# The last eight tap positions of a 31-tap convolution summed on GpSimd instead of VectorE

## The reference, cut to what matters

```python
ca, cb = jnp.split(cv, 2, axis=-1)          # 256 channels each
u = ca * jax.nn.sigmoid(cb)
u = causal_dwconv(u, cv_dw_w) + cv_dw_b      # CV_K = 31 taps, one weight per channel and tap
y_cv = jax.nn.silu(layernorm(u, cv_ln_g, cv_ln_b))
return jnp.concatenate([y_attn, y_dn, y_cv], axis=-1) @ w_out
```

## Time and profile before

| | |
|---|---|
| time, median of 3 runs | 1764.81 us (1764.64 to 1769.44) |
| the profiled execution | 1773.58 us, of which the span from first to last instruction is 1771.5 us |
| busy | TensorE 1600.8 us (90%), VectorE 1188.2 (67%), ScalarE 809.9 (46%), GpSimd 60.5 (3%) |
| mean granted TensorE clock | 0.928 of full speed |
| token mixer of layer 0, tile 9 to the output projection | about 164 to 331 us |
| the same of layer 1 | about 926 to 1094 us |

### The profile page before, as it was taken

How to read it: one execution, slowest core, us unless ns; L and a number is a source line. 1 busy time by engine, 2 the same in 40 slices (tenths; PEclk the granted TensorE clock), 3 DMA queues, 4 the chain that set the end, 5 groups by cost and what they waited for, 6 DMA issues and landing times.

```text
span 1771.5 us, 22310 instructions
## 1 busy us (share of the span) xinstructions
PE 1600.8 (90%) x8914; PEld 1243.6 (70%) x8914; DVE 1188.2 (67%) x1376; ACT 809.9 (46%) x936; POOL 60.5 (3%) x49
## 2 busy tenths in 40 slices
PE   6899978897999998998999788958999999999992
PEld 5467756675888886884677556657888888888882
DVE  4677785477666664444657854256888888888884
ACT  2344226323222222122452254246777777777773
POOL 6200000000000000000000000020000000000001
PEclk9799988798999998998999977968999999999996
DMA  7253220153656554431211100538999999999974
GB/s 312 94 175 116 81 96 1 38 201 95 183 177 186 179 183 136 139 137 36 71 50 43 54 1 4 184 120 294 381 390 392 393 380 392 392 393 384 391 292 154
DMA packets 93718, 341.89 MB, mean 193 GB/s; under 512 B 9904, under 2 KB 14000, under 8 KB 90928
## 3 DMA queue, kind: packets, MB, share of 16 engines
q1 hardware_dynamic: 91312, 332.09, 52.1%
q0 software_dynamic: 2304, 8.39, 1.3%
HBM read 318.42 MB, written 22.02 MB: 192 GB/s over the span
## 4 chain that ended last, share of the span: by engine, by line
PE 79%; DVE 11%; ACT 4%; issue 2%; DMA 2%; POOL 1%; SPq 0%; DVEq 0%; ACTq 0%; POOLq 0%
PE ps L599 33%; PE ps L1101 10%; PE ps L1099 9%; PE ps L1100 9%; DVE scr L1520 5%; PE ps L585 2%; DVE scr L1517 1%; PE ps L914 1%; PE ps L571 1%; ACT whi L1133 1%; PE ps L888 1%; PE ps L745 1%; PE ps L628 1%; PE ps L578 1%; DVE wlo L1527 1%
## 5 line engine op out<-in xcount | busy, mean ns | idle before, releaser
L599 PE MATMUL ps<-hhi,whi 128*128 128x512 f32 x768 | 324.1, 422 | 8.1 <-DVE hlo L1520 8.0
L1527 DVE TENSOR_TENSOR wlo<-raw,whi 128x1024 fp32r<-128x1024 f32 (+1 forms) x114 | 147.1, 1291 | 252.0 <-ACT whi L1133 250.1
L599 PE MATMUL ps<-hhi,wlo 128*128 128x512 f32 x768 | 309.8, 403 | 0.0
L599 PE MATMUL ps<-hlo,whi 128*128 128x512 f32 x768 | 308.5, 402 | 0.0
L1517 DVE TENSOR_TENSOR wlm<-rawm,hlo 128x2048 fp32r<-128x2048 f32 x120 | 274.8, 2291 | 42.5 <-ACT hlo L1414 40.8
L1133 ACT ACTIVATE whi<-raw 128x1024 fp32r<-128x1024 f32 (+1 forms) x114 | 125.7, 1103 | 358.4 <-PE ps L599 357.3
L1414 ACT ACTIVATE hlo<-rawm 128x2048 fp32r<-128x2048 f32 x120 | 230.0, 1918 | 81.5 <-PE ps L1101 81.5
L599 PEld LDWEIGHTS ps<-hhi,whi 128*128 128x128 f32 x768 | 147.9, 193 | 77.3 <-issue 31.4
L1100 PE MATMUL ps<-wlm,xgh 128*128 128x512 f32 x480 | 188.3, 392 | 0.0
L599 PEld LDWEIGHTS ps<-hlo,whi 128*128 128x128 f32 x768 | 147.9, 193 | 35.9 <-issue 3.9
L599 PEld LDWEIGHTS ps<-hhi,wlo 128*128 128x128 f32 x768 | 147.5, 192 | 35.3
(11 more groups left out here) (291 smaller groups left out, 2388.5 us busy)
## 6 DMA issues: line engine op xcount, KB each, us to landing
rawm<-in_wm SPq DMA_DIRECT2D x360, 512.0 KB, 7.4
raw<-in_w SPq DMA_DIRECT2D x98, 512.0 KB, 3.5
adah<-in_ada SPq DMA_DIRECT2D x56, 512.0 KB, 4.3
scr<-in_ada SPq DMA_DIRECT2D x20, 1024.0 KB, 5.8
raw<-in_w SPq DMA_DIRECT2D x16, 704.0 KB, 4.1
xs<-scr SPq DMA_DIRECT2D x15, 512.0 KB, 5.4
xg<-xs SPq DMA_DIRECT2D x15, 512.0 KB, 7.4
ys<-yb SPq DMA_DIRECT2D x15, 512.0 KB, 9.1
```

The source lines that it names most:

```text
L599: ins = pe.matmul(ps[:, b, :], a, r[:, k0 + k, :], start=(start and first and k == ks[0] and n == 0), stop=(stop and last and k == ks[-1] ...
L1527: dve.tensor_tensor(wlo[:, slot, 0:width], raw[:, slot, 0:width], whi[:, slot, 0:width].bitcast(F32), ALU.subtract).then_inc(sem("lo_ready ...
```

## The change

`LATE_TAPS` = 23 splits the taps. VectorE keeps the taps d = 0 to 22 (46 instructions a layer), in a list of that length and with calls `taps(m)` of other sizes. GpSimd takes d = 23 to 30. It can't multiply and add with a tensor in one instruction as written here, so each tap beyond the first is a product into unit 16 (`tensor_scalar` with the channel's weight) and an addition to unit 15 (`CP`), for both sides in turn: 16 products and 14 additions a layer, each behind a semaphore `late_tap` of the ones it depends on. It starts when both PSUM banks of tiles 8 and 9 are free, so when `UT` is whole, and in layer 0 also when the last modulation group of this stretch is summed, since units 15 and 16 are its buffer. VectorE adds `CP` to `CY` once, for both sides together, in half step 1, behind its own last tap. The sync queue waits for that addition (`late_added`) before it loads modulation group 13 into units 15 and 16, ahead of the output projection's tiles.

```diff
--- before.py
+++ after.py
@@ -337,6 +337,7 @@
         KT, VT = side(unit(21), 0), side(unit(21), 1)
         ON = side(unit(21), 1)
         UT, CY, ZT = unit(22), unit(23), unit(24)
+        CP = unit(15)
         ROTT = side(unit(25), 0)
         VTOK = side(unit(25), 1).rearrange("p (n d) -> p n d", n=4)
         R8, LN8, G8, Z8, T8, X8 = (side(unit(n), a)[0:8] for n, a in ((24, 0), (24, 1), (25, 0), (25, 1), (23, 0), (22, 0)))
@@ -347,6 +348,7 @@
         mx, negm, rsum, esk, rden = ([small[:, 80 + 16 * n + 8 * a:88 + 16 * n + 8 * a] for a in range(2)] for n in range(5))
         nsink = small[:, 160:168]
         STEPS = 16
+        LATE_TAPS = 23
 
         def scale_of(k):
             return cole[:, :, k, :].rearrange("p m h -> p h m").unsqueeze(3).broadcast_to([P, 4, 4, 64])
@@ -442,6 +444,8 @@
                     load_ada(G_IN + 3)
             for n in range(DC):
                 load_tile(N_IN_TILES + n + 2)
+                if n == 1:
+                    sp.wait_ge(sem("late_added"), 1)
                 load_ada(G_GATE + n)
             for i in range(FC):
                 for j in range(2):
@@ -539,6 +543,27 @@
                                         ALU.add, ALU.min))
                 pool.tensor_scalar(ang[:, n, :], ang[:, n, :], -float(np.float32(3.1415925)), None, ALU.max)\
                     .then_inc(sem("ang_ready"), 1)
+
+            for layer in range(DEPTH):
+                if layer == 0:
+                    pool.wait_ge(sem("ada_acc"), summed(G_IN + 3))
+                for j in range(2):
+                    pool.wait_ge(sem(f"bank_free{j}"), U_IN[layer] + 5)
+                for d in range(LATE_TAPS, CV_K):
+                    for n in range(2):
+                        o, src = side(CP, n), side(UT, n)
+                        w = PR("cconv", (layer * 2 + n) * CV_K + CV_K - 1 - d)
+                        at = (2 * (CV_K - LATE_TAPS) - 1) * layer * 2 + 4 * (d - LATE_TAPS) - 2 * (d > LATE_TAPS)
+                        first = d == LATE_TAPS
+                        if not first:
+                            pool.wait_ge(sem("late_tap"), at - 1 + n)
+                        out = o if first else side(unit(16), n)
+                        pool.tensor_scalar(out[:, d:], src[:, :S - d], w, None, ALU.mult).then_inc(sem("late_tap"), 1)
+                    for n in range(2):
+                        if d > LATE_TAPS:
+                            o = side(CP, n)
+                            pool.wait_ge(sem("late_tap"), at + 1 + n)
+                            pool.tensor_tensor(o[:, d:], o[:, d:], side(unit(16), n)[:, d:], ALU.add).then_inc(sem("late_tap"), 1)
 
             pool.wait_ge(sem("xs_cleared"), 16 * NB)
             pool.wait_ge(sem("slots_ready"), 1)
@@ -1703,7 +1728,7 @@
                     link(tt(q, q, cosb[:]))
                     mark(tt(q, q, ROTT, ALU.add), "roped")
 
-                tap_list = [(d, n) for d in range(CV_K) for n in range(2)]
+                tap_list = [(d, n) for d in range(LATE_TAPS) for n in range(2)]
 
                 def taps(m):
 
@@ -1714,7 +1739,7 @@
                         if d == 0:
                             ins = dve.tensor_scalar(o, src, w, PR("cb", layer * 2 + n), ALU.mult, ALU.add)
                         else:
-                            dve.wait_ge(sem(f"tap{n}"), CV_K * layer + d)
+                            dve.wait_ge(sem(f"tap{n}"), LATE_TAPS * layer + d)
                             ins = stt(o[:, d:], src[:, :S - d], w, o[:, d:])
                         ins.then_inc(sem(f"tap{n}"), 1)
 
@@ -1781,16 +1806,13 @@
                         ada_groups((G_IN + 1,))
                     if layer == 0 and t in (6, 9):
                         ada_groups((G_IN + (2 if t == 6 else 3),))
-                    if t >= 10:
-                        taps(3 if t == 13 else 4 if t != 15 else 6)
+                    if 10 <= t < 17:
+                        taps(3 if t == 13 else 4)
                     if t == 13:
                         solved()
                         taps(1)
                     if t == 14:
                         queries_less_absorbed()
-                        taps(2)
-                    if t == 17:
-                        taps(2)
 
                 def maxima(i):
 
@@ -1834,10 +1856,14 @@
                 for i in range(STEPS):
                     maxima(i)
                     if i < 2:
-                        taps(6 if i == 0 else 2 * CV_K)
+                        taps(3)
                     if i == 1:
                         for n in range(2):
-                            dve.wait_ge(sem(f"tap{n}"), CV_K * v)
+                            dve.wait_ge(sem(f"tap{n}"), LATE_TAPS * v)
+                        dve.wait_ge(sem("late_tap"), 2 * (2 * (CV_K - LATE_TAPS) - 1) * v)
+                        ins = tt(cy[:, :, LATE_TAPS:], cy[:, :, LATE_TAPS:],
+                                 CP.rearrange("p (a s) -> p a s", a=2)[:, :, LATE_TAPS:], ALU.add)
+                        mark(ins, "late_added")
                         dve.sem_inc(sem("taps_done"), 1)
                     if i in (2, 4, 6):
                         state(3 + i // 2)
```

## The result

The changed kernel takes 1773.9 us (median of 13 runs, 1770.7 to 1783.25); the kernel before took 1767.24 us beside it (13 runs, 1764.16 to 1772.67). The ratio is 1.0036, with a 95% interval of 1.0021 to 1.0051: 6.4 us slower, between 3.7 and 9.0. The time is inside the range of 1756 to 1775 us and 8 us above the forecast of 1766: the change is a small loss, where "the two cancel" was the likeliest case. Of these 8 us 2.4 are the base: the forecast was added to 1764.81, a median of three runs, where thirteen give 1767.24. One execution of a later experiment (the products-only kernel: 2328.74 us at a granted clock of 0.628, where the others had 0.93) was slow as a whole and is left out of its ratio.

A forecast was written before the change was run, and what follows sets the result against it. VectorE's taps ahead of the mean's matmuls were taken to bound the kernel. A gain of 11.6 us against 12.0 of contention and 1 for the clock made +1.4 on 1764.81, so 1766 us, range 1756 to 1775.

The forecast's parts named there:

- the two cancel: Whole kernel: 12.0 us lost to contention, 11.6 gained, 1 for TensorE's clock, net +1.4 us, 1766 us; chance 0.45.
- What bounds the kernel: End of input projection: VectorE's 18 taps hold the mean's matmuls; added VectorE time between tile 9 and the copy costs fully.
- What it removes: 16 of 62 taps per layer; nine delay the second maximum, 0.64 us each: 5.8 us a layer, 11.6 in all.
- GpSimd and the sync queue: GpSimd's 43 us of work per layer ends at about 212 to 225, wanted at 259; the sync queue's wait costs nothing.
- What GpSimd costs VectorE: From tile 9 on, GpSimd's additions and products delay VectorE: 6.8 us in layer 0, 5.2 in layer 1, 12.0 in sum.
- the overlay of the two orders: GpSimd's order laid over VectorE's up to the copy: 5.7 us in layer 0, 4.2 in layer 1.
- the upper end of 18: Contention on VectorE if its single-operand work suffers too: some 18 us instead of 12.
- The clock: TensorE's longer waits ahead of the turned keys lower its clock: between 0 and 2 us, say 1.
- Rival (c): Slower by the clock: layer 0 loses its early clock return behind the mean, +8.0 us, 1773 us; chance 0.23.
- case (a): The likeliest case, loss 12.0 us against gain 11.6, plus 1 for the clock: +1.4 us, 1766 us; chance 0.45.
- Rival (b): Contention mostly misses: additions fall beside PSUM reads and transposes, loss about 5 us, net -6.6, 1753 to 1758 us; chance 0.25.
- rival (d): Every GpSimd instruction blocks for its whole length, products costing 1.3 us when met: 20 us over (a), 1786 us; chance 0.07.

The follow-up runs named there:

- products-only kernel: Changed kernel without GpSimd's 14 additions a layer, all 16 products kept: 1763.78 us, ratio 0.9974 to the kernel before.
- the filler: 22 unread TensorE matmuls a layer around the attention's half steps: 1765.53 us (ratio 0.9983) in the kernel before, 1763.78 us (0.9965) in the changed kernel.
- additions-only kernel: Changed kernel with GpSimd's products cut to four a layer, then 14 additions in a row: 1780.77 us, ratio 1.0069 to the kernel before.
- the moved taps: Kernel before, all 62 taps on VectorE, 12 a layer moved forward: 1760.01 us, ratio 0.9945; with 22 unread TensorE matmuls a layer 1750.97 us, ratio 0.9898.

## Why the prediction was right or wrong

**What bounds the kernel**: right. VectorE's taps held the mean's matmul, and a microsecond more on VectorE ahead of the copy delays the copy.

**What it removes**: right, 12.0 us where the sum had 11.6. The second maximum came 5.8 us a layer earlier in the sum, 5.7 in the trace of layer 0, and the mean's matmul 6.0 in both layers; it was then released by TensorE's own L939 (the old L914), as said, and neither the last three taps nor the new addition (1.18 us, with 1.2 expected) shows in the time.

**GpSimd and the sync queue**: right that nobody waits. GpSimd ended at 216.3 us; it took 50 us where the prediction had 43 undisturbed.

**What GpSimd costs VectorE**: the mechanism and the two prices held (0.79 to 0.86 us for 0.9, 0.24 to 0.30 for 0.25 to 0.3), and the term was too small all the same, 15.3 us for 12.0. Layer 0's copy came 7.6 us later, not 5.7; layer 1's 4.5, for 4.2; behind each copy 1.6 us, for 1.1 and 1.0. The step that failed is the overlay of the two orders: I let five additions and five products meet something ahead of layer 0's copy, and six additions and ten products had run by then. Most of layer 0's miss of 1.9 us sits on two instructions that layer 1 doesn't have, the operations of tile 10 on the tables `cosb` and `sinb`. In the order of time of before:

```profile
175.35 0.54 DVE L1773 TENSOR_SCALAR cosb<-cosb,cst 128x512 f32<-128x512 f32 x1
175.92 0.49 DVE L1774 TENSOR_SCALAR sinb<-sinb,cst 128x512 f32<-128x512 f32 x1
```

Beside two additions they took 1.44 and 1.33 us (L1798, L1799), 1.7 us more. They read one tensor from SBUF each; the prediction counts them among the work on two operands and names single-operand work only as its upper end, so it doesn't say whether the 5.7 us contain them. VectorE's read of PSUM at 201.67, beside additions, took the same 1.22 us as before. A value between 12 and the upper end of 18 would have been the better middle.

**The clock**: too small, at 1 us for both layers. Rival (c) named its sign, L888 behind the mean at 2.00 us in layer 0, and the profile has it (267.99); it had also named the opposite, layer 1 winning, and that came too, in the same execution. These two are a swap of 5.4 against 6.4 us, and another trace of the change has neither. What stayed is elsewhere, in the stretch from the outputs to the square sum: in both layers together 125.7 to 125.8 us in the three traces of the change, 123.0 and 121.7 in the two of before. The clock and busy time of layer 1's, before and then after (window, its us, then the busy time and count of each engine, the granted clock, DMA share and GB/s):

```profile
1049.50:1106.50 57.00, 48.63 (x329) 38.24 (x327) 24.28 (x44) 28.71 (x60) 0.00 (x0) 0.82 0.02 2
```
```profile
1047.30:1107.10 59.80, 51.18 (x323) 39.41 (x322) 24.03 (x44) 28.86 (x60) 0.00 (x0) 0.77 0.01 2
```

The work is the same (VectorE 24.3 and then 24.0 us, ScalarE 28.7 and 28.9), the clock is 0.77 for 0.82, and 57.0 x 0.82 = 46.7 and 59.8 x 0.77 = 46.0 are nearly the same number of cycles: these 2.8 us are clock. The change adds and removes no computation in this stretch. That it only shifts how TensorE arrives there is argued, not shown; for it speaks that with the filler both kernels have 0.82 in layer 1 and the difference is gone.

**The sum.** 15.3 - 12.0 = +3.3 us from contention and gain; -1.6 from a stretch at lowered clock in layer 0's solve to scores (37.3 to 35.7), which both traces of before have and none of after. On average of three traces after and two before, another 3.5 us lie in the last two stretches and 0.6 in layer 1's copy to solve (one trace of before had 21.6 there, the others of both kernels the slower step). Together 5.8, for 6.4 measured. That lies between case (a), +1.4, and rival (c), +8.0, nearer to (c). Of the miss of 5.0 us, 2.9 are contention (3.3 more of it than predicted, less 0.4 more gain); 1.5 are the clock's by these traces (-1.6, 3.5 and 0.6 make 2.5, with 1 predicted), and 0.6 lie outside what the stretches show. Two terms were too small in the same direction; the time is inside the range because that reached 9 us above the forecast. That the clock's part comes from the change rests on five traces and on the pair with the filler matmuls; how often an execution of either kernel falls into which pattern stays open. Rival (b) needed additions to miss, and ahead of the copies few did; rival (d) is refuted by the products-only kernel (0.24 to 0.30 us a product, not 1.0).

## What to carry to other kernels

Work handed to an engine whose instructions hold up those of the bound one isn't free where that one has no slack: price it by kind of instruction (here about 0.8 us for each two-input addition and 0.3 for each one-input product, even where nobody uses the result) and by how much idle time lies under it. Before handing work away, look for idle time earlier on the same engine; here it took 12 taps of a layer and beat the offload by 14 us by the medians, 16 by the ratios. And where a chain of short waits sets the time, look at the granted clock behind each wait: one and the same stretch, mean to outputs, took 25.0 us at a granted clock of 0.68 and 17.7 at 1.00, and filling the wait ahead of it brought the one to the other.

## What the runs showed of the hardware

Sharing goes by the kind of instruction. In the rows above a two-input GpSimd addition and a VectorE instruction on two SBUF operands exclude each other for about their whole length, in both directions: 2.03 us for a mask of 1.21, and 2.23 for an addition of 1.20. A one-input product, which takes 1.5 to 1.8 us, delays VectorE by 0.24 to 0.30 us on average. The Trainium skill, "SBUF — State Buffer", section "SBUF: two separate sides", says that a VectorE instruction with two SBUF inputs, or one in a two-port mode, and a GpSimd instruction that reads SBUF lock each other out: whichever starts first holds the other up for its whole length. The additions agree with it (1.70 us for a tap of 0.72). The products do not: they cost 3.9 us over 13 of them, and the mask begun 0.30 us inside one kept its 1.21 us. Here the measurement decides. VectorE's operations on `cosb` and `sinb`, with one SBUF tensor each, were held up too; no run here shows in which mode they ran.

Also not expected: a GpSimd product of one input took longer than its addition of two. Where VectorE only read PSUM or transposed beside it, a product took 1.50 us (at 183.71 in the products-only kernel) and an addition 1.20 (at 192.39 in the additions-only kernel). And 22 matmuls that compute nothing, 5.5 us of TensorE's time a layer, made the kernel with the moved taps 9 us faster (1760.0 to 1751.0, each beside a kernel before of 1767.8 and 1768.4) and the changed kernel 10 us faster, while what they gave the kernel before is not clear of nothing (ratio 0.9963 to 1.0003).
